# VectorE adds the two half sums of a modulation vector, and the ones product takes half as many groups

## The reference

```python
def modulation(cond, w_ada, b_ada):
    m = jax.nn.silu(cond) @ w_ada + b_ada          # (1024) @ (1024, 6144)
    return [t[..., None, :] for t in jnp.split(m, 6, axis=-1)]

# second block
c_act = jax.nn.silu(c)
mod = c_act @ ada_w[layer] + ada_b[layer]
sh1, sc1, g1, sh2, sc2, g2 = jnp.split(mod, 6, axis=-1)
shift, scale = jnp.split(c_act @ kv_ada_w + kv_ada_b, 2, axis=-1)
```

## Time and profile before

| | before |
|---|---|
| median of three runs | 1728.53 us |
| the profiled execution's own time | 1730.11 us |
| its span, first to last instruction | 1728.0 us |
| TensorE busy | 1657.7 us (96%) |
| TensorE weight load busy | 1463.7 us (85%) |
| VectorE busy | 1297.0 us (75%) |
| ScalarE busy | 819.7 us (47%) |
| GpSimd busy | 242.8 us (14%) |
| mean granted TensorE clock | 0.987 |
| mean DMA rate | 184 GB/s |

### The profile page before, as it was taken

The page is one execution under the profiler, slowest core; times in us unless marked ns, Lnnn a source line. Parts: engine busy times, 40 slices in busy tenths (PEclk is TensorE's granted clock), DMA queues, the critical chain, the costliest instruction groups (busy, mean ns, idle before and its releaser), DMA issues.

```text
span 1728.0 us, 28177 instructions
## 1 busy us (share of the span) xinstructions
PE 1657.7 (96%) x11542; PEld 1463.7 (85%) x11542; DVE 1297.0 (75%) x1866; ACT 819.7 (47%) x1186; POOL 242.8 (14%) x199
## 2 busy tenths in 40 slices
PE   6999989999999999999999999969999999999999
PEld 3887768788788877986999999969999999799887
DVE  5687863887988878857577777887998968757574
ACT  3333662543224423636554556485635444555352
POOL 0423001011001112440310122013000230030000
PEclk8999999999999999999999999989999999999999
DMA  8734002243565459320347556634998866237552
GB/s 326 273 147 171 2 5 93 98 146 116 187 240 203 178 194 325 126 74 1 122 149 259 210 195 262 217 117 164 342 358 339 334 235 223 71 120 272 193 173 95
DMA packets 46575, 317.83 MB, mean 184 GB/s; under 512 B 5232, under 2 KB 6256, under 8 KB 12272
## 3 DMA queue, kind: packets, MB, share of 16 engines
q1 hardware_dynamic: 45936, 312.68, 50.1%
q0 software_dynamic: 512, 3.35, 0.5%
HBM read 314.96 MB, written 1.05 MB: 183 GB/s over the span
## 4 chain that ended last, share of the span: by engine, by line
PE 81%; DVE 10%; ACT 3%; issue 2%; POOL 2%; DMA 1%; SPq 0%; DVEq 0%; ACTq 0%
PE PM L1680 19%; PE PM L1681 19%; PE PM L1682 19%; PE PM L1834 5%; PE PM L1836 3%; PE PM L1964 2%; DVE wlo L1055 2%; PE PX L2000 1%; DVE acc L1089 1%; PE PX L1873 1%; PE PO L2026 1%; PE PX L1930 1%; DMA raw<-in_ada 1%; PE PX L1653 1%; PE PO L2015 1%
## 5 line engine op out<-in xcount | busy, mean ns | idle before, releaser
L1055 DVE TENSOR_TENSOR wlo<-raw,whi 128x2048 fp32r<-128x2048 f32 (+2 forms) x199 | 437.6, 2199 | 74.8 <-ACT whi L733 74.4
L1680 PE MATMUL PM<-H,whi 128*128 128x256 f32 (+1 forms) x1526 | 480.4, 315 | 10.1 <-DVE H L1481 3.0
L1681 PE MATMUL PM<-H,whi 128*128 128x256 f32 (+1 forms) x1526 | 476.7, 312 | 0.0
L1682 PE MATMUL PM<-H,wlo 128*128 128x256 f32 (+1 forms) x1526 | 476.5, 312 | 0.0
L733 ACT ACTIVATE whi<-raw 128x2048 fp32r<-128x2048 f32 (+3 forms) x204 | 365.6, 1792 | 147.4 <-PE PM L1836 43.3
L1680 PEld LDWEIGHTS PM<-H,whi 128*128 128x128 f32 x1526 | 291.5, 191 | 34.4 <-issue 9.3
L1682 PEld LDWEIGHTS PM<-H,wlo 128*128 128x128 f32 x1526 | 291.7, 191 | 16.4
L1681 PEld LDWEIGHTS PM<-H,whi 128*128 128x128 f32 x1526 | 291.8, 191 | 16.0
L1089 DVE SCALAR_TENSOR_TENSOR acc<-raw,silc,acc 128x512 f32<-128x512 f32 x328 | 245.1, 807 | 5.3 <-DMA raw<-in_ada 4.2
L1680 PE MATMUL PM<-G,whi 128*128 128x256 f32 (+1 forms) x608 | 192.7, 317 | 1.7 <-DVE X L1239 1.6
L1682 PE MATMUL PM<-G,wlo 128*128 128x256 f32 (+1 forms) x608 | 190.7, 314 | 0.0
(11 more groups left out here) (243 smaller groups left out, 2668.5 us busy)
## 6 DMA issues: line engine op xcount, KB each, us to landing
raw<-in_ada SPq DMA_DIRECT2D x104, 1024.0 KB, 5.5
raw<-in_wm SPq DMA_DIRECT2D x93, 1024.0 KB, 5.1
raw<-in_wl SPq DMA_DIRECT2D x68, 1024.0 KB, 5.1
raw<-in_wl SPq DMA_DIRECT2D x32, 704.0 KB, 4.2
raw<-in_wm SPq DMA_DIRECT2D x5, 768.0 KB, 4.7
raw<-in_wm SPq DMA_DIRECT2D x4, 704.0 KB, 4.0
X<-in_x SPq DMA_DIRECT2D x1, 2048.0 KB, 13.0
bias<-in_bias POOLq DMA_DIRECT2D x1, 2048.0 KB, 11.1
```

Of the source, the lines that this page charges most:

```text
L1055: dve.tensor_tensor(wslot(wlo, i, usize(u)), slot_raw(n, usize(u)), wslot(whi, i, usize(u)).bitcast(F32), ALU.subtract)\
L1680: pe.matmul(out, st_hi, mv_hi, start=first, stop=False)
L1681: pe.matmul(out, st_hi, mv_lo, start=False, stop=False)
L1682: return pe.matmul(out, st_lo, mv_hi, start=False, stop=last)
```

## The change

For vectors 8 to 25 VectorE, after the second part of a half, waits for the last instruction on both accumulators and adds the second into the first (128 partitions by 512 columns), with a semaphore `whole` of its own. `ada_rows` waits for `whole` of both halves in place of `raw_used`, and multiplies only the first accumulators: four matmuls of 256 columns, not eight. The release of the raw slot stays with the last multiply-add. Vectors 0 to 7 are as before.

```diff
@@ in ada(a), after the loop over the four blocks
                         else:
                             ins.then_inc(*C.link("dve_chain"))
                         marks[half] = C.last
+                if part == 1 and not two:
+                    dve.wait_ge(*marks[0])
+                    dve.wait_ge(*marks[1])
+                    first, second = (acc[:, hv % 2 * 1024 + h * 512:hv % 2 * 1024 + h * 512 + 512] for h in range(2))
+                    dve.tensor_tensor(first, first, second, ALU.add).then_inc(*tick("whole", hv))
@@ in ada_rows(v)
                 for hv in (2 * v, 2 * v + 1):
-                    pe.wait_ge(*at("raw_used", RAW_AT["ada", 2 * hv + 1]))
-                for part in range(1 if v < CTXV else 2):
-                    for r in range(4):
-                        a, w = (r * 512, 512) if v < CTXV else (r // 2 * 1024 + part * 512 + r % 2 * 256, 256)
-                        ins = pe.matmul(dst[32 * r:32 * r + 32, 0:w], ones[:, 0:32], acc[:, a:a + w], start=(part == 0),
-                                        stop=(v < CTXV or part == 1))
+                    pe.wait_ge(*(at("raw_used", RAW_AT["ada", 2 * hv + 1]) if v < CTXV else at("whole", hv)))
+                for r in range(4):
+                    a, w = (r * 512, 512) if v < CTXV else (r // 2 * 1024 + r % 2 * 256, 256)
+                    ins = pe.matmul(dst[32 * r:32 * r + 32, 0:w], ones[:, 0:32], acc[:, a:a + w], start=True, stop=True)
                 ins.then_inc(*tick("aux", key))
```

More of the change, by code:

```diff
@@ L353 @@
               "negm", "rec", "p", "pt_act", "pt_dve", "ptr", "pv", "snk", "snkx", "o", "ocs", "ocr", "ocss", "ocsd", "ocn",
-              "cv1", "cvd", "silu", "prod", "ghi", "glo", "lg", "lx", "lxd", "lr", "la", "lm", "ls", "lh", "ly", "zn", "adap", "score", "sadd", "cstdma", "rowsdma", "mixdma", "biasdma", "cmb",
+              "cv1", "cvd", "silu", "prod", "ghi", "glo", "lg", "lx", "lxd", "lr", "la", "lm", "ls", "lh", "ly", "zn", "adap", "whole", "score", "sadd", "cstdma", "rowsdma", "mixdma", "biasdma", "cmb",
               "act_chain", "dve_chain", "pool_chain", "outd", "prep", "prepa"]
```

## The result

The changed kernel takes 1736.22 us (median of nine runs, 1735.45 to 1739.57); the kernel before, over nine runs, 1730.95 (1728.43 to 1734.06). The ratio is 1.0034, 95% interval 1.0025 to 1.0043: slower by 5.9 us, 4.3 to 7.4. The difference of the medians is 5.3 us. The forecast of 1731.8 was made from a median of 1728.53, as +3.3 us. So the sign was right, and the size was some 2.6 us too small. Its mean granted clock was 0.982, against 0.987 in the profiled execution before.

What follows compares the result with a forecast made beforehand. TensorE was taken to bound the kernel (81% of the chain of waits, VectorE 10%). 17 felt additions at 0.73 us, 12.4, less 9.1 gave +3.3 us, 1731.8 us from a median of 1728.53; range 1724 to 1740.

Steps and rivals of the forecast that it cites:

- p: Price of one VectorE addition on the path: 0.73 us, bounded by about 0.45 and 1.79.
- 18, 21, 25: Vectors with 0.08 us margin at the product, first addition taken up by idle time: p - 0.52, +0.21 us each.
- 22, 23: Vectors whose idle time takes up only part of the first addition: 2p - 1.05 = +0.41 and 2p - 0.87 = +0.59 us.
- What it takes off TensorE: Product of ones, vectors 8 to 25: 8 records for 16, 0.44 us each, 7.9 us if nothing waits.
- The addition: On VectorE, 36 of 692 ns, each starting 0.04 us after the last multiply-add and ending 0.73 after it; 26 us.
- 17p - 9.1: Whole sum: 17 of 36 additions felt, less 9.1 us given by TensorE and taken up by idle times; +3.3 us.
- The rule that a semaphore costs nothing extra: On VectorE, the pipe empties before the next instruction anyway; p would be 0.61 and the sum +1.3 us.
- Which vectors have room: Margins between VectorE's end and the product: above 2 us at 8, 9, 10, 19, 20, 24, small or none elsewhere.
- The stretch from 11 to 13: Unit 43 to the next norm, VectorE setting the pace: 5p - 0.88 = +2.8 us.
- The loads rival: Delayed splits make loads late at vectors 17 to 23, 0.7 us each: +5 on top, 1737 us; chance 0.15.
- All on the path: Rival: VectorE has no room anywhere, so every addition is felt: +18.4 us, 1747; chance 0.07.
- the unshortened product: Rival: TensorE's product doesn't get shorter by half, as if set by weight loads: +10.3 us, 1739; chance 0.04.

Runs made afterwards that it cites:

- swap: The changed kernel with the two waits ahead of each addition in the other order; 1737.47 us against 1729.88 for the kernel before, ratio 1.0041.
- product_only: The changed kernel without VectorE's additions, the short product kept (output wrong); 1722.90 us against 1729.88 for the kernel before, ratio 0.9962.
- stretch: The kernel before with addition and short product for vectors 11, 12 and 13 only; 1736.09 us against 1730.45, ratio 1.0034.
- w1s: The kernel before with addition and short product for vectors 17, 18, 21, 22, 23 and 25 only; 1733.70 us against 1730.45, ratio 1.0020.
- six: The kernel before with addition and short product for vectors 8, 9, 10, 19, 20 and 24 only; 1727.12 us against 1729.88, ratio 0.9980.
- add_only: The changed kernel with its additions but the product of all eight matmuls (output wrong); 1742.51 us, ratio 1.0072 to the kernel before.

## Why the prediction was right, and what in its size was not

The forecast said slower by 3.3 us and gave 1724 to 1740; it came out slower by 5.9, and nearly all of the places and waits were as foreseen. The terms, as forecast with p = 0.73 and as the traces of after and of swap have them (us; lateness gained from the last TensorE instruction ahead of the product to the first behind it, and for 11 to 13 from behind vector 10's product to the norm):

```
vectors                 forecast      after                swap
8, 9, 10, 19, 20, 24    -0.44 each    -0.43 each           -0.43 each
11 to 13, to the norm   +2.8          +4.53                +5.57
14, 15                  0.0, +0.15    +0.07, +0.20         0.00, +0.13
16                      +0.73         +0.80                +0.73
17                      +0.66         +0.84                +0.70
18, 21, 25              +0.21 each    +0.34, +0.34, +0.41  +0.21, +0.22, +0.27
22, 23                  +0.41, +0.59  +0.56, +0.76         +0.41, +0.61
sum                     +3.3          +6.3                 +6.3
of it, clock behind 12                1.4                  2.8
```

swap has its two waits in the order that gives the forecast's p of 0.73, and its terms are the forecast's to 0.06 us, but for the stretch in which its clock fell: without that loss its sum is 3.5. In after it is 4.9. The two profiled executions of before and after differ by 9.5 us, 3.2 more than the sum: after was 2.06 us late at vector 8's product already, and in the attention behind vector 24 it lost some 2.2 us where its clock fell (0.71 from 1490 to 1500 us, 1.00 there before), and elsewhere it was somewhat earlier again. So that 6.3 comes near the 5.9 of the times is in part luck, as the clock's share is that of one execution.

- **What it takes off TensorE** was right: 8 records for 16, 0.57 us to the next matmul where 0.56 was forecast. product_only measured the whole of it, -7.0.
- **The addition** was right in its length (692 ns, from the row of the same form) and wrong in the gap in front of it. "It starts 0.04 after that one's end" was read from an instruction with one wait; the change puts two ahead of it. The trace of before didn't show this form. With p = 0.80 the sum 17p - 9.1 is +4.5 and not +3.3. This term of the sum, p, was mis-sized: 0.73 forecast, 0.80 measured; swap, with the waits in the other order, has the 0.73.
- **The rule that a semaphore costs nothing extra** (the Trainium skill, VectorE: DVE Perf Modes, The DRAIN you can't avoid) would have made the sum +1.3. The measured gaps go the other way: 0.08 us before the end without a wait, 0.03 after it with one, 0.10 after it with the outstanding wait in front. Its section measures copies, and no run here has these.
- **Which vectors have room** was right for all 18. The waits forecast were 0.65 at 18, over 2 at 12, 1.1 at 17, and none at 19; measured 0.70, 3.20, 1.21 and none.
- **The stretch from 11 to 13** by its own formula, 5p - 0.88, gives +3.1 with p = 0.80, and the kernel stretch has 3.15. (The row at 669.42 names 'issue' and not TensorE as what ended VectorE's idle time; that the lateness is passed on there is what stretch bears out.) The other 1.4 us in after are the clock behind vector 12's wait. This term was missing: the prediction priced idle time of TensorE at its length. How much of it is in the median of after no run tells; 4.5 and 1.4 make the 5.9.
- **The loads rival** (+5 more, 1737) gives a time near the measured one, so the traces must decide. ScalarE's waits for loads, in us, times and the longest, before:

```profile
ACT whi L733 <- DMA raw<-in_wl: 35.1, 13, 6.1
ACT whi L733 <- DMA raw<-in_wm: 31.7, 16, 5.2
```

and after:

```profile
ACT whi L733 <- DMA raw<-in_wl: 27.8, 10, 5.8
ACT whi L733 <- DMA raw<-in_wm: 27.6, 13, 4.1
```

66.8 us became 55.4, so the loads are no later than before; as this total is 58.8 in stretch and 48.5 in w1s, no more should be read from it. What decides is the period of vector 19, which this rival wanted at 24.7: it is 1286.10 - 1262.11 = 23.99 us, by the forecast 24.0.
- **All on the path** (+18.4) is out by six, which got faster, and by product_only and add_only together.
- In the prediction's shares, half of late loads (0.075), all on the path (0.07) and the unshortened product (0.04) add up to 0.185, not 0.17; nothing hangs on it.

What stays open: why the clock fell behind the same wait in four traces and not in a fifth, how often it does so in executions that weren't profiled, and the upper part of the time of stretch. The forecast's base was also 2.4 us lower than the median of nine runs, which is no step of the argument.

## What to carry to other kernels

Count the places where work that is moved to a less busy engine is felt, not the share of that engine: here 17 of 36 additions of 0.8 us ate up a real gain of 7 us, while 6 vectors gained all of theirs, and the same edit in 12 chosen places, with the product moved some matmuls back in half of them, is 4.3 us faster. Price an instruction with the form of wait that it will have, and look in the trace at which of two waits stands in an instruction of its own: here it was the one written second, so the wait that ends last belongs first. Idle time of TensorE may cost more than its length. And before a fall of the clock in one trace is put down to a change, look at the same place in traces of kernels that do the same there.

## What the runs showed of the hardware that I had not expected

- VectorE starts an instruction 0.08 us before the end of the last when there is no wait, 0.034 after it when it carries the outstanding wait itself, and 0.104 after it when that wait stands in an instruction before it. Of two waits the one written first is carried by the instruction.
- The granted clock fell to 1.2 GHz behind a TensorE wait of 3.1 to 3.2 us in four of the five traces that have it, for some 3.6 us in after, at a price of 1.4 to 2.8 us, and in none of the six traces with a wait of 1.6 us there.
- With the wait filled, the clock was kept there (1.00). At the next norm, 684 to 700 us, its mean was 1.00, 0.89, 0.82 or 0.79 in different traces, and w1s and before, which do the same work up to there, had 1.00 and 0.89, 1.24 us apart.
- The mean granted clock of a whole execution of the kernel before ran from 0.982 to 0.989, and 0.001 of it went with some 1.05 us.
